# An attention stage on one core: the bias from scaled queries, sums for two heads at once, and another order of the score segments and of the fold

## The reference

```python
def block_attention(q, k, v):                      # blocks of Q_BLOCK = 128 queries
    scale = HEAD_DIM ** -0.5
    def one_block(qblk):
        s = jnp.einsum('bkgqd,bskd->bkgqs', qblk, k).astype(jnp.float32) * scale
        p = jax.nn.softmax(s, axis=-1).astype(v.dtype)
        return jnp.einsum('bkgqs,bskd->bkgqd', p, v)
...
keys = jnp.concatenate([rope_2d(ka), ctx_k.astype(ka.dtype)], axis=1)   # latent: 2048 + 128 keys
att = block_attention(rope_2d(qa), keys, vals)
att = block_attention(qa, ka, va)                                       # context: its own 128 keys
```

## Time and profile before

| | |
|---|---|
| time, median of 3 runs | 3138.7 us (3138.42 to 3140.06) |
| the profiled execution | 3139.49 us |
| its span | 3137.8 us |
| TensorE busy | 2974.2 us (95%) |
| its weight loads busy | 2739.5 us (87%) |
| VectorE busy | 1852.7 us (59%) |
| ScalarE busy | 1674.1 us (53%) |
| GpSimd busy | 700.5 us (22%) |
| attention: first scores to last exponential | 619.6 to 1545.7 us |

### The profile page before, as it was taken

How to read it: one execution, slowest core, us unless ns; L and a number is a source line. 1 busy time by engine, 2 the same in 40 slices (tenths; PEclk the granted TensorE clock), 3 DMA queues, 4 the chain that set the end, 5 groups by cost and what they waited for, 6 DMA issues and landing times. The chain is left out here.

```text
span 3137.8 us, 57856 instructions
## 1 busy us (share of the span) xinstructions
PE 2974.2 (95%) x20880; PEld 2739.5 (87%) x20880; DVE 1852.7 (59%) x3261; ACT 1674.1 (53%) x3227; POOL 700.5 (22%) x878
## 2 busy tenths in 40 slices
...
GB/s 256 84 68 68 68 60 203 178 14 35 17 30 20 17 33 17 20 30 17 45 208 148 120 96 201 188 194 189 194 197 189 196 196 189 191 199 195 194 184 285
DMA packets 320130, 394.76 MB, mean 126 GB/s; under 512 B 30260, under 2 KB 276488, under 8 KB 319016
## 3 DMA queue, kind: packets, MB, share of 16 engines
...
q10 hardware_dynamic: 384, 0.62, 0.1%
...
## 5 line engine op out<-in xcount | busy, mean ns | idle before, releaser
L2877 DVE TENSOR_TENSOR e_w_lo<-e_raw,e_w_hi 128x2048 fp32r<-128x2048 f32 x189 | 433.1, 2291 | 411.7 <-ACT e_w_hi L2794 411.7
L92 PE MATMUL e_ps<-e_x_hi,e_w_hi 128*128 128x272 f32 x2048 | 601.6, 294 | 2.6 <-issue 2.6
L94 PE MATMUL e_ps<-e_x_hi,e_w_lo 128*128 128x272 f32 x2048 | 593.4, 290 | 0.0
L93 PE MATMUL e_ps<-e_x_lo,e_w_hi 128*128 128x272 f32 x2048 | 590.0, 288 | 0.0
L1709 DVE TENSOR_TENSOR a_pT_lo<-a_ps_t,a_pT_hi 128x512 fp32r<-128x512 f32 (+1 forms) x648 | 367.8, 600 | 137.2 <-ACT a_pT_hi L1618 136.9
L1618 ACT ACTIVATE a_pT_hi<-a_ps_t 128x512 fp32r<-128x512 f32 (+1 forms) x648 | 319.3, 532 | 160.2 <-PE a_ps_t L1486 155.1
L92 PEld LDWEIGHTS e_ps<-e_x_hi,e_w_hi 128*128 128x128 f32 x2048 | 386.3, 189 | 3.0 <-issue 3.0
L93 PEld LDWEIGHTS e_ps<-e_x_lo,e_w_hi 128*128 128x128 f32 x2048 | 387.0, 189 | 0.0
L94 PEld LDWEIGHTS e_ps<-e_x_hi,e_w_lo 128*128 128x128 f32 x2048 | 385.8, 188 | 0.0
L2794 ACT ACTIVATE e_w_hi<-e_raw 128x2048 fp32r<-128x2048 f32 x189 | 360.6, 1908 | 0.0
L1486 PE MATMUL a_ps_t<-ident,a_prob 128*128 128x128 f32 x2184 | 329.6, 280 | 29.9 <-DVE a_pT_lo L1709 19.1
...
## 6 DMA issues: line engine op xcount, KB each, us to landing
...
```

What stands on the lines that cost most here:

```text
L92: nc.tensor.matmul(out, w_hi, x_hi, start=first, stop=False)
L93: nc.tensor.matmul(out, w_hi, x_lo, start=False, stop=False)
L94: return nc.tensor.matmul(out, w_lo, x_hi, start=False, stop=last)
L2877: nc.vector.tensor_tensor(w_lo[n % RING][:, :, :], raw[n % RING][:, :, :], w_hi[n % RING][:, :, :].bitcast(F32), ALU.subtract).then_inc(w_ ...
```

## The change

Four things, all in attention.

1. The queries are multiplied by minus the scale (-1/8) when they are split: the ScalarE copy gets `scale=-SCALE`, VectorE's subtraction becomes a scalar_tensor_tensor. The scores come out negative and scaled; VectorE takes minima in place of maxima, and the minimum of the three minima is the bias as it stands. The instruction at line 1692 and its semaphore are gone; the exponential is exp(-1 * score + bias).
2. Row sums and reciprocals are made for two heads at once, in odd steps only; `a_sums` has room for four heads.
3. `SEG_ORDER` is [2, 0, 1]. The small segment is the first on all three engines: its scores stand between turns 2 and 3 on TensorE, its exponential is the first, its extreme is taken between turns 1 and 2 on VectorE.
4. The fold stands ahead of turn 4 on TensorE, and the combine ahead of low part 4 on VectorE.

```diff
-PE_STEP = [("turn", 0), ("turn", 1), ("value", 0), ("value", 1), ("turn", 2), ("turn", 3), ("scores", 0), ("value", 2),
-           ("scores", 2), ("turn", 4), ("fold", 0), ("scores", 1)]
+PE_STEP = [("turn", 0), ("turn", 1), ("value", 0), ("value", 1), ("turn", 2), ("scores", 2), ("turn", 3), ("scores", 0),
+           ("value", 2), ("fold", 0), ("turn", 4), ("scores", 1)]
...
-SEG_ORDER = [0, 2, 1]
+SEG_ORDER = [2, 0, 1]
...
-                          "turn": lambda n: n in turns_of(i), "total": lambda n: True,
+                          "turn": lambda n: n in turns_of(i), "total": lambda n: h % GROUP == GROUP - 1,
...
-                nc.scalar.activation(q_parts[:, :, 0, :], q_row[:, :, :], ACT.Copy).then_inc(q_hi_ok, 1)
+                nc.scalar.activation(q_parts[:, :, 0, :], q_row[:, :, :], ACT.Copy, scale=-SCALE).then_inc(q_hi_ok, 1)
...
-                    if not (isinstance(n, int) and n < 2):
-                        act.wait_ge(sum_ok, n - 1)
+                    if not (isinstance(n, int) and n < 2 * GROUP):
+                        act.wait_ge(sum_ok, i * NGRP + h // GROUP - 1)
                 nc.scalar.activation(seg_probs(i, h, seg), seg_scores(seg, seg_width(i, seg)), ACT.Exp,
-                                     bias=nm[:, h % 2:h % 2 + 1], scale=scale,
-                                     accum_out=sums[:, h % 2, seg:seg + 1]).then_inc(exped[seg], 1)
+                                     bias=nm[:, h % 2:h % 2 + 1], scale=-1.0,
+                                     accum_out=sums[:, h % (2 * GROUP), seg:seg + 1]).then_inc(exped[seg], 1)
...
-                nc.vector.tensor_tensor(q_parts[:, :, 1, :], q_row[:, :, :], q_parts[:, :, 0, :].bitcast(F32),
-                                        ALU.subtract).then_inc(q_lo_ok, 1)
+                nc.vector.scalar_tensor_tensor(out=q_parts[:, :, 1, :], in0=q_row[:, :, :], scalar=-SCALE,
+                                               in1=q_parts[:, :, 0, :].bitcast(F32), op0=ALU.mult, op1=ALU.subtract)\
+                    .then_inc(q_lo_ok, 1)
...
-                nc.vector.tensor_reduce(mx[:, h % 2, seg:seg + 1], seg_scores(seg, seg_width(i, seg)), AXY, ALU.max)\
+                nc.vector.tensor_reduce(mx[:, h % 2, seg:seg + 1], seg_scores(seg, seg_width(i, seg)), AXY, ALU.min)\
                     .then_inc(max_ok, 1)
                 if seg == segs_of(i)[-1]:
                     dve.wait_ge(max_ok, (n + 1) * 3 if not (isinstance(i, int) and i == NT) else NT * NQ * 3 + h + 1)
-                    nc.vector.reduce_max(mx[:, h % 2, 3:4], mx[:, h % 2, min(segs_of(i)):3], AX).then_inc(max_all, 1)
-                    dve.wait_ge(max_all, n + 1)
...
-                    nc.vector.tensor_scalar(nm[:, h % 2:h % 2 + 1], mx[:, h % 2, 3:4], -scale, None, ALU.mult)\
+                    nc.vector.tensor_reduce(nm[:, h % 2:h % 2 + 1], mx[:, h % 2, min(segs_of(i)):3], AX, ALU.min)\
                         .then_inc(nmax_ok, 1)
...
-                nc.vector.reduce_sum(total_s[:, h % 2:h % 2 + 1], sums[:, h % 2, min(segs_of(i)):3], AX).then_inc(sum_ok, 1)
-                dve.wait_ge(sum_ok, n + 1)
-                nc.vector.reciprocal(rsum[:, h:h + 1], total_s[:, h % 2:h % 2 + 1]).then_inc(rsum_ok, 1)
+                grp = h // GROUP
+                of = slice(grp % 2 * GROUP, (grp % 2 + 1) * GROUP)
+                nc.vector.reduce_sum(total_s[:, grp % 2, :], sums[:, of, min(segs_of(i)):3], AX).then_inc(sum_ok, 1)
+                dve.wait_ge(sum_ok, i * NGRP + grp + 1)
+                nc.vector.reciprocal(rsum[:, grp * GROUP:(grp + 1) * GROUP], total_s[:, grp % 2, :]).then_inc(rsum_ok, 1)
```

More of the change, by code:

```diff
@@ L18 @@
 QPK = NQ // NKV
+SCALE = HD ** -0.5
+assert HD == 64
 NH = NQ + NKV
@@ L1104 @@
 CTX_KEYS = NT + 1
[L1107 to L1109 removed]
+PE_STEP = [("turn", 0), ("turn", 1), ("value", 0), ("value", 1), ("turn", 2), ("scores", 2), ("turn", 3), ("scores", 0),
+           ("value", 2), ("fold", 0), ("turn", 4), ("scores", 1)]
+ACT_STEP = [("keep", 0), ("turn", 0), ("turn", 1), ("exp", 2), ("exp", 0), ("turn", 2), ("turn", 3), ("exp", 1),
             ("turn", 4)]
[L1111 to L1113 removed]
+DVE_STEP = [("turn", 0), ("turn", 1), ("total", 0), ("scores", 2), ("turn", 2), ("turn", 3), ("scores", 0), ("fold", 0),
+            ("turn", 4), ("scores", 1)]
+SEG_ORDER = [2, 0, 1]
 PIECES = [(0, 3), (3, 6), (6, 9), (9, 12), (12, 15), (15, KEY_TILES)]
@@ L1154, in queries_hi @@
         act.wait_ge(self.q_in, 16)
-        self.nc.scalar.activation(self.q_parts[:, :, 0, :], self.q_row[:, :, :], ACT.Copy).then_inc(self.q_hi_ok, 1)
+        self.nc.scalar.activation(self.q_parts[:, :, 0, :], self.q_row[:, :, :], ACT.Copy, scale=-SCALE).then_inc(self.q_hi_ok, 1)
     def keys_hi(self, act, n):
```

15 lines of the change are left out of this document (6 added, 9 removed).

## The result

The changed kernel takes 3104.8 us (median of 4 runs, 3103.83 to 3106.99) against 3139.38 for the kernel before in the same series (4 runs). The ratio is 0.9885 [0.9872, 0.9898]: 34.6 us less, where the forecast was 29.3 less (3110).

What follows compares the result with a forecast made beforehand. No engine simply full: two interlocked rings, ScalarE's and VectorE's, with TensorE waiting for late partners. Step gains of 1.74 a tile times 16 (27.8) plus 1.5 in the context tile, 29.3 off 3139.5, gave 3110 us; range 3095 to 3130.

Steps and rivals of the forecast that it cites:

- Bias, 0.19 off the chain: VectorE: dropping the scaling instruction takes 0.19 us from the chain to low part 0 and the first exponential.
- h=1 cannot be shorter than ScalarE's ring: Step transposing head 1's probabilities, 6.36 us: ScalarE has no idle time from 1.54 to 6.30, so gain 0.
- Transpose 3 at 3.88, 0.22 to spare: TensorE: behind scores 2, transpose 3 starts 3.88 us after the step's start, 0.22 before ScalarE would have to wait.
- rival 4: Slower: transpose 3 behind scores 2 delays segment 1's exponential, 0.15 us in each step, 19 in all, 3159; chance 0.05.
- the threshold of 4.10: ScalarE: if transpose 3 starts later than 4.10 us into the step, ScalarE waits and its ring grows.
- Fold ahead, zero: TensorE: the fold ahead of transpose 4 uses the same bank count and gains zero.
- Bias and segment order together: Attention steps: bias ready at 2.37 us instead of 2.82; gains 0.49 in h=0 and h=2, 0.41 in h=7.
- A new wait of 0.13 at scores 0: TensorE: scores 0 wait 0.13 us because their exponential is now second, done at 4.41 against 4.28.
- rival 1: TensorE's own work becomes the bound in odd steps too; another 1.0 us a tile, 3094; chance 0.08.
- The query split, +0.06 for the instruction: VectorE, h=5: the queries' low part as scalar_tensor_tensor costs 0.06 us more once a tile; step gain 0.35.
- Sums zero, reduces and exponentials of the same duration: Sums lie in VectorE's idle time, alone bringing nothing; changed reduces and exponentials cost zero, each 896-column reduce within -0.02 and +0.05.
- Context tile, 1.5: Context tile: each of eight heads has the bias on its bare path, 8 x 0.19 = 1.5 us gained.

Runs made afterwards that it cites:

- bias_alone: The kernel before with only the scaled queries and the one-instruction bias; 3124.35 us, ratio 0.9939 to the kernel before.
- no_accum: The changed kernel with exponentials that make no row sums (the sums are a constant 1); 3099.45 us, ratio 0.9865 to the kernel before.
- no_fold: The changed kernel with fold and combine back behind transpose 4 and low part 4; 3119.41 us, ratio 0.9925 to the kernel before.
- No_sums: The changed kernel with sum and reciprocal made in every step again; 3101.86 us, ratio 0.9877 to the kernel before.
- q_early: The changed kernel with the next tile's queries split two heads earlier on ScalarE and one on VectorE; 3095.35 us, ratio 0.9851 to the kernel before.
- unrolled: The kernel of q_early with the attention loop over tiles written out; 3091.09 us, ratio 0.9841 to the kernel before.
- no_bias: The changed kernel with the two-instruction bias and unscaled queries back; 3118.9 us, ratio 0.9925 to the kernel before.
- seg_alone: The kernel before with only the small segment moved first on the three engines; 3132.7 us, ratio 0.9968 to the kernel before.
- no_seg: The changed kernel with the segment order 0, 2, 1 back on all engines; 3128.66 us, ratio 0.9961 to the kernel before.
- fold_alone: The kernel before with only fold and combine moved ahead of transpose 4 and low part 4; 3146.21 us, ratio 1.0011 to the kernel before.

## Why the prediction was right, and where it was not

The direction, the time to about 5 us and the main mechanism were right: the low parts came earlier, and TensorE's waits for them fell from 54.1 to 16.8 us. The sum was nevertheless put together partly from the wrong pieces.

- **Bias, 0.19 off the chain: right.** One reduce of 157 ns is left, and bias_alone shows 0.18 to 0.20 in h=0, h=1, h=2, h=5 and h=7.
- **"h=1 cannot be shorter than ScalarE's ring": wrong.** This is the claim that failed most plainly. The ring held a wait for the bias, and bias_alone brings h=1 to 6.17. The Trainium skill, "ScalarE: Activation LUTs", section "What ACT_TABLE_LOAD costs", states that back-to-back ACTIVATEs overlap by about 93 ns; the trace agrees, with about 0.11 us where nothing is waited for and none in the earlier trace rows at 1142.70, so the wait could have been read before the change. That after shows 6.32, near the 6.36 forecast, is the sum of two effects that nearly cancel: 0.19 gained by the bias, 0.15 lost as below.
- **"Transpose 3 at 3.88, 0.22 to spare": wrong, and rival 4's mechanism is there in small.** Transpose 2 starts at 3.19, not 3.13; it and scores 2 take 0.42 and 0.43 (1123.04 between them), not 0.40 and 0.35; transpose 3 starts at 4.04 (1123.47). Also the threshold of 4.10 assumed ScalarE ready at 4.24, and it is ready at 4.06 (1123.49), which puts the threshold near 3.92. So ScalarE's third and fourth high part take 1.22 and not 1.08 in all, and the exponential starts at 5.17 where bias_alone has 4.98. no_accum pins this on transpose 3. It costs 0.15 in h=1 and 0.11 in h=3 (against bias_alone's 6.17), far from the 0.15 in every step of rival 4, since transpose 2 did come earlier.
- **Fold ahead, zero: wrong, the largest mis-sized term.** On top of the rest it brings 13 us: 0.25 in h=4 and 0.13 in h=6, where I had zero, 0.14 to 0.17 of what h=0, h=2 and h=7 gained, and all that h=5 gained (7.18 without it, 7.15 before), which I had credited to the low parts. The step that failed is "same bank count": the count is the same, but the bank is not. I asked what the fold would wait for in its new place (low part 2) and not what it waited for in the old one (low part 3, over at 7.24 in h=4, with the fold's weight load at 7.35), so I took h=4 and h=6 for TensorE's own work. I had also overlooked that the modulation sum of odd steps takes the fold's place.
- **Bias and segment order together: too large.** no_fold, which is what my sum priced, gains 24 us, not 29.3. Its h=7 is 6.49 and its h=0 6.89, where I had 6.36 and 6.69. With the fold both landed on the forecast: right numbers, in part for the wrong reason.
- **A new wait of 0.13 at scores 0: not there.** The exponentials started at 2.51 and not 2.68 (no bias wait), so scores 0 run at 4.35 in h=2 without a wait, and h=2 is TensorE's content, 6.38 for 6.48. That is rival 1's picture, in even steps alone.
- **The query split, +0.06 for the instruction: wrong; h=5 mis-sized.** The new form takes 691 ns and the old one took 690. But it starts 0.22 behind the reduce (1148.41 - 1148.19), where the old one stood 0.10 behind the scale, so of the bias's 0.19 only 0.07 of the way to it remained. h=5 gained 0.22, not 0.35.
- **Sums zero, reduces and exponentials of the same duration: right** (1087 ns for the 896-column reduce, forecast bound +0.05 on the 1080 before).
- **Context tile, 1.5: wrong.** The first exponential of the context tile runs 35.8 us earlier (1487.19 for 1523.01), the first high part of the output projection 36.0 (1518.14 for 1554.09). So the stretch between them takes 31.0 us in place of 31.1: the heads of the context tile gave 0.1. Two effects nearly cancel there. TensorE's clock fell to its half level (1.2 GHz) once more and earlier than before; the stretch after (us, busy of five engines, granted clock, DMA share, GB/s):
```profile
1490.00:1495.00 5.00, 4.06 (x21) 3.83 (x22) 1.06 (x4) 0.90 (x4) 0.00 (x0) 0.67 0.00 0
...
1505.00:1515.00 10.00, 7.21 (x30) 5.77 (x28) 3.38 (x15) 2.74 (x11) 0.00 (x0) 0.50 0.07 27
```
  TensorE had been busy 4.45 of the 5 us before that (1485 to 1490), at full clock. In the kernel before, 1525 to 1536 were granted in full, and half came only then (0.52 in 1536 to 1552, 0.50 in the earlier trace rows). No_sums, q_early, no_accum and unrolled, whose clock did not fall early, take 29.1 to 29.4 us for the same stretch, so the early fall, which the prediction had priced at up to 5 us, cost about 1.6. Without it the gain would have been 1.7, but not from the bias: no_bias, with the two-instruction bias and an undisturbed clock, takes 29.5. It goes with the segment order: seg_alone takes 28.5 and no_seg 31.9. Why an order of segments helps a tile that has one segment wasn't tried. Behind attention the lead shrinks from 36.0 to the span's 34.0, without any experiment on why: from that high part to the end, before takes 1583.7 us, after 1585.6, and the other eleven kernels 1584.5 to 1585.8.

By steps the account closes. Against the forecast the gain is larger by 0.44 in h=4 and h=6 (the fold), by 0.10 in h=2 (no wait at scores 0) and by 0.11 in h=1, h=3 and h=7, and smaller by 0.03 in h=0 and 0.13 in h=5: together 0.49 a tile or 7.8 us, less 1.4 in the context tile and 2.0 behind attention, 4.4 in all. The profile has 34.0 less 29.3, 4.7; the medians have 5.3. Two things that this leaves out nearly cancel: attention's first scores come 1.4 later after (621.02 for 619.65), within the 618.3 to 623.1 of the thirteen traces, and from there to the context tile's first exponential the gain is 37.2, 1.7 more than 16 times 2.22.

That the order of fold and transpose 4 is the cause of 0.2 us in h=4 is shown by fold_alone (7.82 to 7.61) and no_fold (7.75 against 7.50); that it is the wait for low part 3 rests on the times of the weight loads in all these traces and on the kernel's turns of the banks, not on an experiment that moves the banks alone. What stays open: why the query split begins 0.22 behind the reduce, and the two stretches outside the sixteen tiles.
